# Where an expert stage's first chunks lie, and where modulation chunks stand between attention units

## What is computed

```python
mod_x = (silu(c) @ w_mod + b_mod).reshape(-1, 6, d)      # modulation vectors, first block
x = x + mod_x[:, 2] * hybrid_mixer(...)                  # 16 head pairs in two attentions
hx = modulate(rms_norm(x, g_ffn), mod_x[:, 3], mod_x[:, 4])
# expert choice: each of 16 experts takes its 32 best tokens
aff = softmax(hx @ w_router); gate, idx = top_k(aff.T, 32)
xe = hx[idx]
hid = silu(xe @ w_gate) * (xe @ w_up)                    # (32, 1024) per expert
ye = (hid @ w_down) * gate
x = x + mod_x[:, 5] * zeros.at[idx].add(ye)
mod = silu(c_2) @ ada_w + ada_b                          # modulation vectors, second block
x = x + g1 * nsa_mixer(rms_norm(x) * (1 + sc1) + sh1, ...)   # 16 head pairs again
```

## Time and profile before

| | us |
|---|---|
| median of 3 runs | 1718.4 (1718.2 to 1718.93) |
| the profiled execution | 1717.33 |
| its span | 1715.5 |
| PE matmul busy | 1446.0 (84%) |
| DVE busy, ACT busy | 813.4 (47%), 592.2 (35%) |
| q1, the weights' DMA queue | 430.99 MB, 63.2% of 16 engines' span |
| mean granted PE clock | 0.918 of 2.4 GHz |

### The profile page before, as it was taken

One profiled execution on the slowest core, in us unless ns is written; L12 is line 12 of the kernel. 1 busy time (PEld: TensorE's weight loads), 2 busy tenths in 40 slices (PEclk: granted clock), 3 DMA queues, 4 the chain that ended last, 5 costly groups with the idle time before them and its releaser, 6 DMA issues. The chain is left out here.

```text
span 1715.5 us, 26725 instructions
## 1 busy us (share of the span) xinstructions
PE 1446.0 (84%) x11126; PEld 1123.3 (65%) x11126; DVE 813.4 (47%) x1371; ACT 592.2 (35%) x849; POOL 21.8 (1%) x34
## 2 busy tenths in 40 slices
PE   5999998999876665566565699889999999899999
PEld 3889885668752221121121487459999998799999
DVE  4343437666631010101010577555776466977763
ACT  3431135674321101010000342554443355753432
POOL 1100000000000000000000000000000000100000
PEclk8999999999968778777888799999999999899999
DMA  9754357733729999999999754944454544344520
GB/s 397 306 225 193 147 237 272 259 140 114 294 95 430 427 427 429 427 428 427 428 427 428 316 222 168 370 174 148 174 195 173 191 162 164 123 172 175 193 101 25
DMA packets 46909, 437.67 MB, mean 255 GB/s; under 512 B 5200, under 2 KB 5584, under 8 KB 6224
## 3 DMA queue, kind: packets, MB, share of 16 engines
q1 hardware_dynamic: 45792, 430.99, 63.2%
q10 hardware_dynamic: 1008, 5.07, 0.7%
HBM read 434.99 MB, written 1.05 MB: 254 GB/s over the span
## 5 line engine op out<-in xcount | busy, mean ns | idle before, releaser
L732 PE MATMUL bank<-arena_r,ring_r 128*128 128x256 f32 (+1 forms) x5032 | 703.5, 285 | 24.4 <-DVE ring_r L1806 8.9
L732 PEld LDWEIGHTS bank<-arena_r,ring_r 128*128 128x128 f32 x5032 | 655.5, 191 | 41.1 <-issue 28.4
L1806 DVE TENSOR_TENSOR ring_r<-ring,ring_r 128x2048 fp32r<-128x2048 f32 x109 | 249.5, 2291 | 184.3 <-ACT ring_r L1455 184.1
L1101 PE MATMUL bank<-ring,arena 128*32 128x512 f32 x1008 | 167.3, 800 | 124.5 <-DMA ring<-in_w 124.1
L1455 ACT ACTIVATE ring_r<-ring 128x2048 fp32r<-128x2048 f32 x109 | 207.9, 1907 | 126.8 <-PE bank L732 117.7
L1101 PEld LDWEIGHTS bank<-ring,arena 128*32 128x32 f32 x1008 | 34.0, 129 | 246.3 <-DMA ring<-in_w 145.2
L732 PE MATMUL bank<-H_r,ring_r 128*128 128x256 f32 x816 | 182.6, 289 | 4.6 <-DVE H_r L1783 4.6
L2073 DVE TENSOR_TENSOR arena<-arena,bank 64x512 f32<-64x512 f32 x16 | 11.1, 691 | 278.0 <-ACT arena L1565 278.0
L732 PEld LDWEIGHTS bank<-H_r,ring_r 128*128 128x128 f32 x816 | 137.3, 196 | 7.9 <-issue 7.4
L1565 ACT ACTIVATE arena<-bank 64x512 f32<-64x512 f32 x16 | 9.4, 589 | 367.6 <-PE bank L1101 367.6
L732 PE MATMUL bank<-arena_r,ring_end_r 128*128 128x256 f32 (+1 forms) x384 | 109.8, 286 | 0.0
(11 more groups left out here) (277 smaller groups left out, 1477.8 us busy)
## 6 DMA issues: line engine op xcount, KB each, us to landing
ring<-in_w SPq DMA_DIRECT2D x95, 2048.0 KB, 25.7
ring<-in_w SPq DMA_DIRECT2D x171, 1024.0 KB, 4.9
ring_end<-in_w SPq DMA_DIRECT2D x45, 1024.0 KB, 4.8
ring<-in_bias ACTq DMA_DIRECT2D x1, 2048.0 KB, 12.8
ring_end<-in_w SPq DMA_DIRECT2D x1, 2048.0 KB, 22.3
consts<-in_consts ACTq DMA_DIRECT2D x1, 1183.0 KB, 9.4
X<-in_x SPq DMA_DIRECT2D x1, 1024.0 KB, 5.5
arena<-in_ctx SPq DMA_DIRECT2D x1, 1024.0 KB, 7.9
```

Of the source, the lines that this page charges most:

```text
L732: i = nc.tensor.matmul(o, lhsT, rhs, start=start, stop=stop, skip_group_check=grouped)
L1101: last = matmul(bank[0][32 * j:32 * j + 32, :], x_cur[:, k, :], place(slot_of(c))[:, 512 * j:512 * j + 512], start=k == 0, stop=k == KT - 1)
L1806: v.tensor_tensor(r(lo), lo, r(hi), ALU.subtract).then_inc(lo_ready, 1)
```

## The change

Two things are changed.

**Six places for expert 0's last chunks.** `EARLY` becomes slots 12, 13 and four `home`s outside the ring: 14 in `consts` (columns 384 to 2431, rotation and mask tables of the first block), 15 in the arena, 16 and 17 in the upper and lower half of `H`. Expert 0's chunks 0 to 5 go to ring slots 0 to 5, its chunks 6 to 11 to the six places, chunks 12 to 17 to slots 6 to 11, chunk 18 to slot 0 again. 18 chunks are resident before the stage. The homes are loaded singly, half a pair each; 16 and 17 are written in pieces of 256 elements. SP waits for `merged_ready` before home 14, for all chunks before the experts before home 15, for `sum_sq` 1 before 16 and for the last `tok_major` before 17. The first refills of the ring are written out, since their counts do not follow the loop's rule.

**Units without modulation chunks.** `take_unit` replaces `take(2)` at the head of both attention loops: it takes up to two steps, stops behind a `mod_row`, and takes nothing in the next unit. In the first stage block 5's chunks move one unit later, its `mod_out` two. In the nsa stage blocks 7 and 8 begin two and three units later; the splits of nsa_out 0 and 1, which stood before `mod(8,0)` and `mod(8,1)` in two units, stand before the same steps, now in one unit; `mod_row(8)` moves from unit 13 to 15 and `mod_out(8)` from 13 to 18.

```diff
-SLOTS, CYCLE = 14, 12
+SLOTS, CYCLE, HOMES = 14, 12, 4
+    resting = [False]
+
+    def take_unit():
+
+        if resting[0]:
+            resting[0] = False
+            return
+        for _ in range(min(2, len(fill))):
+            s.append(fill.pop(0))
+            if s[-1][0] == "mod_row":
+                resting[0] = True
+                return
...
     for i in range(PAIRS + LAG + 1):
-        take(2)
+        take_unit()
         if i < PAIRS:
             s.append(("att_s", i))
...
     for i in range(PAIRS + LAG + 1):
-        take(2)
+        take_unit()
         if i < PAIRS:
             s.append(("nsa_s", i))
...
-EARLY = (12, 13)
+EARLY = (12, 13) + tuple(range(SLOTS, SLOTS + HOMES))
 FIRST_CYCLE = FIRST_EXPERT + len(EARLY)
+FIRST_HOME = FIRST_EXPERT + CYCLE - len(EARLY)
...
-                s = EARLY[c - FIRST_EXPERT] if c < FIRST_CYCLE else (c - FIRST_CYCLE) % CYCLE
+                if FIRST_HOME <= c < FIRST_HOME + len(EARLY):
+                    s = EARLY[c - FIRST_HOME]
+                else:
+                    s = (c - FIRST_EXPERT if c < FIRST_HOME else c - FIRST_CYCLE) % CYCLE
             sem_slot = s
-            if FIRST_EXPERT <= c < FIRST_SECOND:
+            if FIRST_EXPERT <= c < FIRST_SECOND and s < SLOTS:
...
+        def home(s):
+            return {14: consts[:, 384:384 + CHUNK], 15: room(8448, CHUNK), 16: H[:, :, T:2 * T], 17: H[:, :, 0:T]}[s]
...
-                with sp_eng.Fori(1, full) as r:
+                for c in range(FIRST_CYCLE + CYCLE, FIRST_CYCLE + 2 * CYCLE, 2):
+                    sp_eng.wait_ge(chunk_used, RING[c + 1][2] + 1)
+                    load_pair(slot_of(c), pair_of(c))
+                with sp_eng.Fori(2, full) as r:
                     for i in range(CYCLE // 2):
...
+            def load_home(s, source):
+                n = CYCLE - len(EARLY) + EARLY.index(s)
+                half = pair_of(FIRST_EXPERT + n - n % 2)[:, n % 2 * CHUNK:n % 2 * CHUNK + CHUNK]
+                sp_eng.dma_start(source, half).then_inc(landed[s], 16)
...
             sp_eng.wait_ge(merged_ready, 4)
+            load_home(14, home(14))
             for s in range(6, CYCLE, 2):
                 load_pair(s, pair_of(FIRST_CYCLE + s))
-            for c in sorted((FIRST_CYCLE, FIRST_CYCLE + 2, FIRST_EXPERT), key=lambda c: RING[c + 1][2]):
+            for c in sorted((FIRST_EXPERT, FIRST_EXPERT + 2, FIRST_HOME), key=lambda c: RING[c + 1][2]):
...
             sp_eng.wait_ge(chunk_used, FIRST_EXPERT)
-            load_pair(RING_USE[1][2][0], pair_of(FIRST_CYCLE + RING_USE[1][2][0]))
+            load_pair(4, pair_of(FIRST_EXPERT + 4))
+            load_home(15, home(15))
+            sp_eng.wait_ge(job_done, JOBS[("sum_sq", 1)].no)
+            load_home(16, home(16))
+            sp_eng.wait_ge(job_done, JOBS[("tok_major", 1, 1)].no)
+            load_home(17, home(17))
             pair_rounds()
```

More of the change, by code:

```diff
@@ L469, in room, with columns @@
             return v
+        def home(s):
+            return {14: consts[:, 384:384 + CHUNK], 15: room(8448, CHUNK), 16: H[:, :, T:2 * T], 17: H[:, :, 0:T]}[s]
+        def columns(s, j, n):
+            if s >= SLOTS + 2:
+                return home(s)[:, n // T * j:n // T * (j + 1), :]
+            return (home(s) if s >= SLOTS else place(s))[:, n * j:n * (j + 1)]
         ident, ones, half_ones = const("ident"), const("ones"), const("half_ones")
@@ L539, in mod_rows @@
             return room(15872, 2 * T) if b == 0 else norm_t[:, b % 2, :]
-        landed = [sem(f"landed{i}") for i in range(SLOTS)]
+        landed = [sem(f"landed{i}") for i in range(SLOTS + HOMES)]
         chunk_used = sem("chunk_used")
@@ L1101, in step_experts @@
                             last = matmul(bank[0][32 * j:32 * j + 32, :], x_cur[:, k, :],
-                                          place(slot_of(c))[:, 512 * j:512 * j + 512], start=k == 0, stop=k == KT - 1)
+                                          columns(slot_of(c), j, 512), start=k == 0, stop=k == KT - 1)
                         last.then_inc(chunk_used if k < KT - 1 else gate_up_done, 1)
@@ L1123, in step_experts @@
                         pe.wait_ge(landed[landed_slot(at)], 16 * landed_count(at))
-                        ck = place(slot_of(at)).rearrange("p (k n) -> p k n", k=2)
                         for kk in range(2):
@@ L1128, in step_experts @@
                                 last = matmul(bank[2][32 * j:32 * j + 32, 0:T],
-                                              hid_t[:, k % 4, k // 4 * CAP:k // 4 * CAP + CAP], ck[:, kk, j * T:j * T + T],
+                                              hid_t[:, k % 4, k // 4 * CAP:k // 4 * CAP + CAP], columns(slot_of(at), 4 * kk + j, T),
                                               start=k == 0, stop=k == KT - 1)
```

## The result

| | us |
|---|---|
| kernel before, median of 4 | 1718.3 (1716.58 to 1718.93) |
| changed kernel, median of 4 | 1700.76 (1699.85 to 1704.44) |
| ratio | 0.9905, 95% interval 0.9891 to 0.992 |
| profiled execution of the changed kernel, its span | 1699.85, 1698.1 |

The account below looks back on a forecast made before the run. DMA refills were taken to bound the expert stage, PE waits the nsa stage. Gains 8.1 + 7 + 1.5 = 16.6 us from 1717.3 gave 1700.7, as a median 1702; forecast 1697 to 1706, range with rivals 1696 to 1711.

Parts of the forecast that it names:

- Part 1: Expert stage: four more chunks loaded ahead gain 9.8 + 1.7 - 3.5 = 8.1 us; bounds 4.6 and 11.5.
- Part 2: Nsa stage: units without modulation chunks; terms sum to 7.6 us, taken as 7; bounds 0 and 11.
- (a): Nsa stage: the 2.81 us wait for norm_t and slow matmuls behind it go, 4.2 us; 1.5 come back, 2.7 taken.
- (b): Nsa stage: the 3.36 us wait for norm_t and slow groups behind it go, 4.7 us; 4.1 taken.
- (c): Nsa stage, unit 11: nsa_out 0 and 1 splits together hold DVE 4.6 us; cost 1.0 us, bounds 0 and 4.6.
- (d): Nsa stage's end: six PE waits, 4.7 us, and a slow output group, 1.3 us; moved chunks gain 1.8 us.
- Part 3: First attention stage: moved modulation steps gain 1.5 us, half of two waits totalling 2.9; bounds -1 and +3.
- The mechanism named for gate 6: First attention stage: its 1.60 us wait is for a bank; without modulation transposes ahead, it takes one emptied earlier.
- Rival (A): Nsa stage: waits only move since bare units lack PE work, gain there 0; 1708.8 us, chance 0.15.
- (B): Expert stage: extra chunks give nothing, DMA idle stretch grows to 11.5 us; 1709.9 us, half 1705; chance 0.07 for either.
- (C): Nsa units 3 to 10: PE's clock stays low in units without modulation chunks, +15 us; 1724 us, chance 0.04.
- The half rate that the prediction allowed for: Loads of the two homes in H, 1 KB pieces: at half rate 4.9 us a megabyte, within the cover; cost 0.

Follow-up runs that it names:

- e4_two_places: Changed kernel with two homes outside the ring in place of four, 16 chunks resident: 1705.22 us, ratio 0.9925.
- e5_again: Changed kernel with slots 12 and 13 used once more, for the fourth refill, once chunk 7 of expert 0 is used: 1701.48 us, ratio 0.9916.
- e8: Changed kernel with slots 12 and 13 used again, nsa_out 1's split one unit later and nkv 1's split held back: 1696.9 us, ratio 0.9887.
- e10: Like e8, but the unit after a modulation row is no longer left without modulation chunks: 1697.35 us, ratio 0.9888.

## Why the prediction was right, point by point

**Part 1** was forecast at 8.1 us and is 8.6 in the whole change and 8.0 alone. Each term of the sum is seen: the first refill 1.86 us earlier relative to expert 0 (1.71 forecast), the idle stretch of 3.5 us, and two pairs less. The fourth refill's wait for chunk 13 was the right thing to price, as `e4_two_places` and `e5_again` show from both sides. The four single loads cost nothing, as said: the first was issued at 439.64 and landed at 444.78, the other three landed at 482.56, 485.36 and 490.43, and the first refill was issued only at 506.60. The end of the stage cost nothing either: behind the last pair, landed at 941.50, the second block's first chunks followed every 2.5 us.

**Part 2** was forecast at 7 us and is 5.7; its inner terms were less good than their sum. (a) 2.7 forecast, with 1.5 us coming back: one wait of 0.86 came back, so 3.3. (b) 4.1 forecast, 4.1 found: a wait of 0.60 in the bare unit. (c) 1.0 forecast: the two splits in one piece cost waits of 1.81, 0.15 and 0.28 us and 3.4 us of slow groups, 5.6 in all, where the kernel before had one wait of 0.55, so 5.1. This is the mis-sized step. I had compared DVE's chain (9 us) with PE's work ahead of it (7.5) and got the wait nearly right (1.5 for 1.8), but left out the lower clock behind the wait, although I had counted exactly that in (a) and (b). The upper bound, 4.6, was too low for the same reason.

(d) 1.8 forecast, 2.8 found, of which 1.1 are waits and 1.7 the clock, which stayed at 1.00 to the end. The waits of 1.13, 0.60 and 0.74 stayed, where I had hoped for half. Whether the chunks among the last units keep the clock up isn't shown. Behind the same waits of 1.13 and 0.60 us the same output group was slow in all three traces with the old order, quick in nine with chunks moved there, and slow in two more of these, `e8` and `e10`, whose nsa stages took 80.26 and 79.65 us for it (the changed kernel, then `e8`):

```profile
1133.79 1.52 PE L771 MATMUL bank<-H,arena 128*64 128x256 f32 x16
```

```profile
1127.65 1.05 PE L783 MATMUL bank<-consts,arena 128*15 128x128 f32 x8 [1.13 <-DVE arena L2246]
1129.30 0.75 PE L779 MATMUL bank<-arena 15*64 15x256 f32 x4 [0.60 <-ACT H L1683]
1129.97 2.83 PE L779 MATMUL bank<-H,arena 128*64 128x256 f32 x16
```

The four terms as found add up to 5.1; the 0.6 that is missing are slow groups behind the two old waits, 0.3 us behind each, that (a) and (b) had not counted. The modulation transposes of block 8 stand in unit 17, not 18, which changes nothing in this.

**Part 3** was forecast at 1.5 and is 2.0 in the stage, of which 1.3 us were gone again before the experts. The mechanism named for gate 6 fits, no wait is left there; of the 1.27 us before the transposes 0.70 stayed. The loss behind the stage was in no step, and over all traces only 0.4 to 0.7 us of part 3 are left at the squares' sum.

**Not forecast**: 1.6 us gained ahead of the nsa stage, and 0.4 between the experts and nkv. The first is again the clock: both kernels wait 2.34 us for DVE before the compression scores (before, then after):

```profile
1061.37 1.96 PE L732 MATMUL bank<-arena 64*32 64x512 f32 x16 [2.34 <-DVE arena L2126]
1063.26 2.64 PE L732 MATMUL bank<-ring,silu_c 128*32 128x512 f32 x16
```

```profile
1051.30 1.09 PE L771 MATMUL bank<-arena 64*32 64x512 f32 x16 [2.34 <-DVE arena L2164]
1052.32 1.92 PE L771 MATMUL bank<-ring,silu_c 128*32 128x512 f32 x16
```

Behind the same wait the same work runs at either rate. The total came within 1.3 us of the forecast partly by luck: parts 2 and 3 fell 2.0 us short, and part 1's 0.5 and 2.3 us found in no part made up for it. Within part 2, (c) was 4.1 us too small; (a), (d), the slow groups not counted and the 0.6 us that I had taken off the sum gave back 2.8 of these. Rival (A) did not happen, (B) did to the size that the sum had for it, and (C) happened only behind the splits, not in the bare units: the windows with units 4 and 10 in them, 1066 to 1075 and 1075 to 1109, have a clock of 1.00.

## What to carry to other kernels

Where a stage is bound by DMA, count when each refill may be issued, not only how much is loaded ahead: a place outside the ring saves its bytes but frees nothing, and the four places outside the ring, two pairs of 4.9 us of DMA each, gave 6.8 us (with the earlier first refill) and 1.7 us. A planner that derives the place of a step from a slot table will move steps when the table changes; list every step that moved before pricing the change, and look at the next stage when a gain doesn't arrive. Price a wait of PE with the clock behind it: the waits of 2.81 and 3.36 us had 1.7 and 1.6 us of slower groups behind them, the 2.2 us behind the two splits had 3.4, and one of 1.13 had 1.7 or nothing.

## What the runs showed of the hardware

The granted clock after a wait isn't a function of the wait's length alone. The same waits of 1.26 and 0.81 us were followed by 1.00 in three traces and by 0.79 over 8 us in the others looked at; one of 2.34 us, and one of 1.13 with 0.60 behind it, were followed by either, with the same group after them. A difference of 1.5 us between two single traces of this kernel means nothing until the clock in the same windows has been compared.

A megabyte on an idle DMA queue pays for its start, and little for small pieces. Home 17 was written to SBUF in 1 KB pieces; its windows in the changed kernel, from 486 on, have 95, 282, 386 and 286 GB/s:

```profile
487.00:488.00 1.00, 0.00 (x0) 0.00 (x0) 0.93 (x4) 0.00 (x0) 0.00 (x0) 0.50 0.93 282
488.00:489.00 1.00, 0.00 (x0) 0.00 (x0) 0.93 (x4) 0.00 (x0) 0.00 (x0) 0.50 1.09 386
```

That is some 3.7 us where the steady rate of 427 GB/s would need 2.5. But a megabyte loaded alone in 8 KB pieces, in the same trace from 406 on, took 3.4 us (57, 377, 434 and 180 GB/s):

```profile
407.00:408.00 1.00, 1.00 (x11) 1.00 (x10) 0.56 (x1) 0.34 (x1) 0.00 (x0) 1.00 0.91 377
408.00:409.00 1.00, 1.00 (x10) 1.00 (x9) 1.00 (x1) 0.00 (x0) 0.00 (x0) 1.00 1.03 434
```

So the pieces cost about 0.3 us and the start about 1 us. Home 16, in the same pieces but behind running transfers, landed 2.8 us after home 15. The half rate that the prediction allowed for did not come up.
